# Expert outputs of a routed layer are weighted on the chip and scattered with an add into the output rows

## The reference

```python
def hier_moe(xn, w_router_group, w_router_expert, w_gate, w_up, w_down):
    t = xn.reshape(-1, D_MODEL)
    lg = (t @ w_router_group).astype(jnp.float32)
    g = jnp.argmax(lg, axis=-1)                       # one of 4 groups
    p_g = jnp.max(jax.nn.softmax(lg, axis=-1), axis=-1, keepdims=True)
    le = (t @ w_router_expert).astype(jnp.float32).reshape(-1, N_GROUPS, EXPERTS_PER_GROUP)
    le_g = jnp.einsum('nge,ng->ne', le, jax.nn.one_hot(g, N_GROUPS, dtype=jnp.float32))
    top_v, top_i = lax.top_k(le_g, TOP_K_IN_GROUP)    # two of its 8 experts
    w_sel = jax.nn.softmax(top_v, axis=-1) * p_g
    ...
    def expert_step(acc, ew):
        wg, wu, wd, cw = ew
        h = jax.nn.silu(t @ wg) * (t @ wu)
        return acc + cw[:, None] * (h @ wd).astype(jnp.float32), None
...
    return h + hier_moe(rms_norm(h, g_norm_ffn), ...)
```

## Time and profile before

| | us |
|---|---|
| median of 3 runs | 599.04 |
| profiled execution | 603.15 |
| its span | 601.5 |
| PE busy (TensorE, matmuls) | 552.0 (92%) |
| DVE (VectorE) | 278.9 (46%) |
| ACT (ScalarE) | 168.3 (28%) |
| POOL (GpSimd) | 156.6 (26%) |

### The profile page before, as it was taken

One profiled execution on the slowest core, in us unless ns is written; L12 is line 12 of the kernel. 1 busy time (PEld: TensorE's weight loads), 2 busy tenths in 40 slices (PEclk: granted clock), 3 DMA queues, 4 the chain that ended last, 5 costly groups with the idle time before them and its releaser, 6 DMA issues.

```text
span 601.5 us, 8410 instructions
## 1 busy us (share of the span) xinstructions
PE 552.0 (92%) x2972; PEld 322.4 (54%) x2972; DVE 278.9 (46%) x694; ACT 168.3 (28%) x386; POOL 156.6 (26%) x187
## 2 busy tenths in 40 slices
PE   6999999999999989999999999999987878789993
PEld 4798899897675655553555944333332223233321
DVE  5887677978314899614458631111210111111245
ACT  7445343423302647622322210100110000000013
POOL 0488788410001187610000021121110111100003
PEclk9999999999999999999999798999998899999998
DMA  7990332589586920049805759999999999999856
GB/s 277 278 289 24 121 145 79 182 250 310 180 210 200 405 104 2 3 138 392 350 35 212 278 177 379 409 420 419 421 422 420 423 417 422 420 421 419 349 225 244
DMA packets 48199, 163.48 MB, mean 272 GB/s; under 512 B 8666, under 2 KB 22042, under 8 KB 36872
## 3 DMA queue, kind: packets, MB, share of 16 engines
q1 hardware_dynamic: 41344, 144.93, 64.1%
q0 software_dynamic: 6528, 17.01, 7.8%
q10 hardware_dynamic: 288, 1.05, 0.4%
HBM read 151.06 MB, written 19.76 MB: 284 GB/s over the span
## 4 chain that ended last, share of the span: by engine, by line
PE 47%; DMA 16%; SPq 11%; DVE 7%; issue 3%; POOL 3%; ACT 3%; DVEq 0%; POOLq 0%; ACTq 0%
PE bank L1129 10%; DMA ring<-in_w_up_dram 10%; PE bank L1061 9%; SPq L533 8%; PE bank L1156 4%; DMA x<-q_rows 3%; SPq L546 3%; DMA ring<-results 2%; PE bank L1012 2%; PE bank L831 2%; POOL ring L2188 2%; PE bank L926 2%; PE bank L809 2%; PE bank L832 2%; PE bank L836 2%
## 5 line engine op out<-in xcount | busy, mean ns | idle before, releaser
L1129 PE MATMUL bank<-ring,work 128*64 128x512 f32 x512 | 121.2, 629 | 18.3 <-DMA ring<-in_w_up_dram 18.3
L1129 PEld LDWEIGHTS bank<-ring,work 128*64 128x64 f32 x512 | 39.7, 144 | 96.5 <-issue 82.4
L1506 DVE TENSOR_TENSOR work<-work,bank 128x256 f32<-128x256 f32 x16 | 6.7, 421 | 135.1 <-ACT work L1441 135.1
L752 PE MATMUL bank<-split 128*128 128x384 f32 x192 | 66.1, 344 | 0.1
L1156 PE MATMUL bank<-ring,work 128*64 128x512 f32 x256 | 58.5, 598 | 7.6 <-ACT work L1445 7.6
L753 PE MATMUL bank<-split 128*128 128x384 f32 x192 | 64.3, 335 | 0.0
L2255 POOL DMA_INDIRECT work<-hn_rows,tbl x15 | 15.2, 1016 | 107.7 <-PE bank L1139 92.4
L1441 ACT ACTIVATE work<-bank 128x256 f32<-128x256 f32 x16 | 6.1, 384 | 131.1 <-PE bank L1129 131.1
L1061 PE MATMUL bank<-ring 128*128 128x512 f32 x96 | 42.6, 595 | 0.0
L2188 POOL TENSOR_TENSOR ring<-ring 128x192 f32<-128x192 f32 (+1 forms) x40 | 38.8, 989 | 7.9 <-DVEq L1601 6.8
L2263 POOL DMA_INDIRECT results<-work,tbl x15 | 15.0, 1001 | 99.0 <-DVE work L2033 99.0
(11 more groups left out here) (277 smaller groups left out, 873.2 us busy)
## 6 DMA issues: line engine op xcount, KB each, us to landing
ring<-in_w_down_dram SPq DMA_DIRECT2D x32, 1024.0 KB
ring<-in_w_gate_dram SPq DMA_DIRECT2D x28, 1024.0 KB
ring<-in_w_up_dram SPq DMA_DIRECT2D x28, 1024.0 KB
ring<-in_w_in_dram SPq DMA_DIRECT2D x7, 1536.0 KB, 11.3
results<-work POOLq DMA_DIRECT2D x1, 4160.0 KB, 24.5
x<-in_x_prompt_dram SPq DMA_DIRECT2D x8, 512.0 KB, 15.7
ring<-in_w_out_dram SPq DMA_DIRECT2D x2, 2048.0 KB, 16.1
ring<-in_w_gate_dram SPq DMA_DIRECT2D x8, 512.0 KB, 20.6
```

Source lines behind the costliest of these rows:

```text
L752: pe.matmul(bank[n % 3][:, 0:CW], xT_high[:, k, cols], w_high[c][:, k, :], start=(k == 0), stop=False)
L1129: last = pe.matmul(bank[2][64 * h:64 * h + 64, :], xgT[:, k, 64 * h:64 * h + 64], gate_up[s][h][:, :, k, :], start=(k == 0), stop=(k == KD ...
L1506: return dve.tensor_tensor(out, a, b, op)
```

## The change

The output rows take the sum themselves. SyncE writes `x` (that is `h`) to the output right after it is complete, behind the weights of pair 2 and ahead of those of pair 3. VectorE and ScalarE multiply by the slot's weight while they copy a pair's result out of its banks. GpSimd then scatters those rows straight into the output with an add, by two indirect DMAs for a pair: one into the 512 prompt rows, which skips the sample tokens, and one into the 8 sample rows, which skips all others. Word 1 of the table is now the row in the sample output.

An add that goes out while another one to the same row is on its way would be lost. Two things prevent that. A pair now holds the experts `i` and `i + 16`, which lie in different groups, so that no token stands twice in one pair. And the scatter of a pair waits until that of the pair before has landed, and the first one until the rows of `h` have landed.

The weights of all 16 pairs' slots come from one matrix product (`weigh`, 16 columns in place of 1), which both copies of pair 0 now wait for. What goes: the tensor `results` with its clearing, its reading back, the sums of VectorE, ScalarE and GpSimd at the end, the matrix `holder` and its matmuls, the four dummy matmuls and two `own_row` products behind pair 13, and the special treatment of pair 15. The loops of VectorE and ScalarE over the pairs are written out. The weights' requests are the same DMAs in the same order, for other experts. The overflow branch is rewritten too.

```diff
@@ SyncE
-            gates((4, 5), 2, (1,))
+            gates((2, PAIRS + 2), 2, (1,))
+            for m, t in enumerate(ORDER):
+                sp.wait_ge(S["h_done"], m + 1)
+                sp.dma_start(y_rows[t] if t < NT else ys_rows, x[0:TILES[t], t, :]).then_inc(S["y_out"], 16)
+            third = (3, PAIRS + 3)
             sp.wait_ge(S["pair_half"], 1)
-            half_gates((6, 7), 0, 0, gu_in[0])
+            half_gates(third, 0, 0, gu_in[0])
...
-            combine_rows(1)
@@ TensorE
-                        last = pe.matmul(bank[7][:, 0:1], in_slot[:, i, m, :], weigh_by[:, i, m:m + 1],
+                        last = pe.matmul(bank[7][:, 0:PAIRS], in_slot[:, i, m, :], in_pair[:, i, m, :],
...
-                if i == 13:
-                    own_row(SUMMED[0], 0)
-                    own_row(SUMMED[0], 1)
-                    keep_warm(4, bank[3])
@@ ScalarE
-                act.wait_ge(S["dn_done"], i + 1)
-                act.activation(yo[s][:, 0:512], bank[4][:, :], ACT.Copy).then_inc(S["dn_evac_a"], 1)
+                if landed is not None:
+                    act.wait_ge(res_sem[s], landed)
+                else:
+                    act.wait_ge(S["tbl_ready"], 4)
+                if split:
+                    act.wait_ge(S["pair_half"], 2)
+                else:
+                    act.wait_ge(S["dn_done"], i + 1)
+                act.activation(yo[s][:, 0:512], bank[4][:, :], ACT.Copy, scale=weight).then_inc(S["dn_evac_a"], 1)
@@ VectorE
-                dve.tensor_copy(yo[s][:, 512:D], bank[5][:, :]).then_inc(S["dn_evac_v"], 1)
+                dve.tensor_scalar(yo[s][:, 512:D], bank[5][:, :], weight, None, ALU.mult).then_inc(S["dn_evac_v"], 1)
@@ GpSimd
-            pool.wait_ge(S["v_used"], 2)
-            pool.memset(xg[0], 0.0).then_inc(S["zero_rows"], 1)
-            clear_results(1)
...
-            def scatter(i, s, choices):
+            def add_rows(s, tokens, decoded):
+
+                for out, at, n in ((y_prompt[0], tokens, SEQ), (ys_rows, decoded, DEC)):
+                    pool.indirect_dma_start(out, bass.IndirectOffsetOnAxis(at, 0), yo[s], None, bounds_check=n - 1,
+                                            oob_is_err=False, compute_op=ALU.add).then_inc(res_sem[s], 16)
+
+            def scatter(i, s):
 
                 pool.wait_ge(S["dn_evac_a"], i + 1)
                 pool.wait_ge(S["dn_evac_v"], i + 1)
+                if i >= 1:
+                    pool.wait_ge(res_sem[(i - 1) % 3], 32 * ((i - 1) // 3 + 1))
                 pool.sem_inc(S["moved_go"], 1)
-                pool.indirect_dma_start(results, bass.IndirectOffsetOnAxis(choices, 0), yo[s], None,
-                                        bounds_check=CHOICES - 1, oob_is_err=False).then_inc(res_sem[s], 16)
+                add_rows(s, tbl[:, 0, i:i + 1], tbl[:, 1, i:i + 1])
...
-            pool.wait_ge(S["scattered"], 16)
-            for i in range(PAIRS - 1):
+            pool.wait_ge(S["y_out"], 16 * (NT + 1))
+            for i in range(PAIRS):
                 if i + 4 < PAIRS:
                     pool.wait_ge(S["xg_turned"], 2 * i + 4)
                     gather((i + 1) % 3, tbl[:, 0, i + 4:i + 5])
-                scatter(i, i % 3, tbl[:, 1, i:i + 1])
+                scatter(i, i % 3)
```

More of the change, by code:

```diff
@@ L588, in _ @@
                     i = 3 * j + 6 + s
-                    expert(2 * i, 2 * i + 1, s, i)
+                    expert(i, i + PAIRS, s, i)
             sp.wait_ge(S["gu_done"], PAIRS - 3)
-            half_gates((30, 31), 0, 0, S["front_in"])
-            half_gates((30, 31), 0, 1, gu_in[0])
+            half_gates((PAIRS - 1, E - 1), 0, 0, S["front_in"])
+            half_gates((PAIRS - 1, E - 1), 0, 1, gu_in[0])
             sp.wait_ge(S["dn_done"], PAIRS - 3)
[L594 to L608, removed]
-            combine_rows(1)
+            downs((PAIRS - 1, E - 1), 0)
             sp.wait_ge(S["flag_ready"], 1)
@@ L1166, in _ @@
             weigh()
-            with pe.Fori(0, 4) as j:
+            for i in (1, 2, 3):
+                s = i % 3
+                pair(i, s, i // 3 + 1, False)
+                turn_tokens(i + 1, (s + 1) % 3, 16 * (i // 3 + 1))
+                pair_down(i, s, i // 3 + 1, False)
+            with pe.Fori(0, 3) as j:
                 for n, s in enumerate((1, 2, 0)):
-                    i = 3 * j + 1 + n
-                    turn = j + 1 + (1 if s == 0 else 0)
+                    i = 3 * j + 4 + n
+                    turn = j + 2 + (1 if s == 0 else 0)
                     pair(i, s, turn, False)
-                    turn_tokens(i + 1, (s + 1) % 3, 16 * (j + 1) + (16 if s == 0 else 0))
+                    turn_tokens(i + 1, (s + 1) % 3, 16 * (j + 2) + (16 if s == 0 else 0))
                     pair_down(i, s, turn, False)
-            def own_row(t, half):
-                pe.matmul(sum_bank(t, half)[:, :], ident[:, :], x[:, t, half * 512:(half + 1) * 512], start=True, stop=False)
             for i in range(13, 16):
@@ L1183, in _ @@
                     turn_tokens(i + 1, (s + 1) % 3, 80)
-                else:
-                    own_row(SUMMED[1], 0)
                 pair_down(i, s, i // 3 + 1, False, i == PAIRS - 1)
-                if i == 13:
-                    own_row(SUMMED[0], 0)
-                    own_row(SUMMED[0], 1)
-                    keep_warm(4, bank[3])
[L1192 to L1195, removed]
-                for half in range(2):
-                    if m == 0:
-                        pe.wait_ge(S["dn_evac_v" if half else "dn_evac_a"], PAIRS)
-                    if t == 3:
-                        pe.wait_ge(*((S["h_done"], T5 + 1) if half else (S["add_read"], 1)))
-                    pe.matmul(sum_bank(t, half)[0:TILES[t], :], holder[:, t, 0:TILES[t]], yo[0][:, half * 512:(half + 1) * 512],
-                              start=(t not in SUMMED), stop=True).then_inc(S["added"], 1)
             pe.wait_ge(S["flag_ready"], 1)
@@ L1868, in read_ranks @@
                 for m in range(m0, m1):
-                    at_ = chain.put(tt(place_in[:, m, :], rank(b, m - m0)[:, 0:2], away[:, m, :], ALU.add))
+                    at_ = chain.put(tt(place_in[:, m, :], rank(b, m - m0)[:, 0:E:PAIRS], away[:, m, :], ALU.add))
                 for m in range(m0, m1):
@@ L2042, in _ @@
-            with dve.Fori(0, 3) as j:
-                for n, s in enumerate((1, 2, 0)):
-                    i = 3 * j + 4 + n
-                    hidden(i, False)
-                    tokens(i + 1)
-                    result(i, s, 16 * (j + 1) + (16 if s == 0 else 0))
-            for i in range(13, 15):
-                hidden(i, False)
-                tokens(i + 1)
-                if i == 14:
-                    for t in range(T5):
-                        dve.tensor_scalar(holder[:, t, :], iota128, float(t * P), last_token, ALU.add, ALU.is_equal)\
-                            .then_inc(S["slot_ready"], 1)
-                result(i, i % 3, 16 * (i // 3))
```

206 lines of the change are left out of this document (65 added, 141 removed).

## The result

The kernel after takes **603.62 us** (median of 11 runs, 601.16 to 606.21); the kernel before, run beside it, took 598.43 (11 runs). The ratio is 1.0095, 95% interval 1.0067 to 1.0122: slower by about 0.9%. The forecast was 602.7 us and 0.6% slower. Two of the 12 executions of the kernel with the clearing put back (611.84 and 899.29 us) and one of the 12 of the kernel before with its clearing later (2542.65 us) were in a slow state, of which the cause isn't known, and the ratios leave them out.

What follows compares the result with a forecast made beforehand. The DMA engines were taken to bound the pairs' stage. Tail -10.1, clock +1.2, add +10.9, skipped rows +1.0 and rows of `h` +0.7 gave +3.7 us, a median of 602.7 us; range 591.5 to 613, 8 in 10.

Steps and rivals of the forecast that it cites:

- What bounds the kernel: Pairs' stage, 352 to 568 us: DMA engines always busy at 410 GB/s, so bytes added there lengthen the kernel in full.
- The add: Pairs' scatters: an add costs one row time more, 13 x 0.65 x 1.28 = +10.9 us (0 to 21.8).
- The tail: Behind the last down product: copy, scatter, landing and 0.8 us closing, new end 591.4, -10.1 us (-12 to -9).
- TensorE's clock: Pair 14's gate and up: without the dummies 8.78 us, not 7.09; partly covered by waiting, +1.2 us (0 to 1.7).
- Skipped rows: Scatters into the sample rows: skipping nearly all 128 slots, 13 times, costs +1.0 us (0 to 2).
- The rows of `h`: Writes of 2.1 MB before pair 3's weights: idle engines at 341 to 351 us hide them, +0.7 us (0 to 4).
- At nothing: Parts put at no cost: the clearing, pair 0's copies waiting for `weigh`, scaled copies, GpSimd's second issue, written-out loops.
- The chain of scatters: Rival, chance 0.10: each scatter waits for the one before; at 16 us a cycle the time is 616.
- The sum: Whole kernel: -10.1 + 1.2 + 10.9 + 1.0 + 0.7 = +3.7 us, span 605.2, median 602.7 us, 0.6% slower.

Runs made afterwards that it cites:

- The run with SyncE's wait: The kernel after, with the wait for the last scatters moved from GpSimd to the end of SyncE's program: 601.12 us, ratio 1.0035.
- the doubled writes: The kernel after, with the rows of `h` written once more, 2.1 MB to a spare tensor: 605.53 us, ratio 1.0099.

## Why the prediction was right, by its steps

**What bounds the kernel** held. Taking the add out shortened the stage by 10.8 us, which is no less than what it took of the engines ahead of pair 14's weights (13 x 0.73 = 9.5 us), and making TensorE faster in pair 14 left the stage as long as it was (238.80 us against 238.70).

**The add** (+10.9) is the term that decided, and its size was right: 10.8 us of stage between the two traces, 9.9 to 10.9 with the other traces. Its factors were each a little off: 0.73 us for a scatter, not 0.65. With 13 scatters that is 9.5 us of the mean engine, so the factor for the busiest one would be 10.8/9.5 = 1.14 and not 1.28, if the whole 10.8 are the add's. No run measured that factor by itself.

**The tail** (-10.1) was wrong by half: -4.7. I had the last landing at 590.6, 8.5 us behind the last down product, and the end 0.8 later. What it measured behind that product: the first scatter issued at +1.7, forecast +1.6; the second one issued 1.85 after it, because an issue with an add takes 1.55 us; the landing of that one 4.3 us after its issue, shorter than the 6.93 that I took from the copy, and than my lower end of 5, for which I had shown no row; then 6.8 us of closing for 0.8. The step that failed is "the span ends at 601.5, so 0.8 us": I read the closing of before, where GpSimd was done with its sums at 588.40 + 4.99 = 593.39 and could take its branch while others worked, as a property of the end, though the change puts the flag and the branch behind the last landing. The run with SyncE's wait shows 4.0 us of it; the 2.0 us by which the other 2.8 exceed my 0.8 stay open.

**TensorE's clock** (+1.2): pair 14 took 9.81 us, more even than 8.78, but a faster one is worth some 0.5 us at most in the runs. I had let only 0.5 us of waiting cover it; where the stage ends by its weights, the next wait takes up all of it.

**Skipped rows** (+1.0): q0's share with copies alone rose from 8.4% to 9.2%, 2.1 us, of which 0.25 MB more, mostly pair 15's rows, are 0.6; the other 1.5 us go with 16 more scatters, like the 1.6 us above. Leaving them out gave 0.7 us in time by the medians. That is within my range of 0 to 2, and too small for the runs to size.

**The rows of `h`** (+0.7): nothing that can be told, as the doubled writes show. `tokens(0)` waited for its tile but started sooner than before, so did pair 3's requests (348.55, was 351.95).

**At nothing.** The copies of pair 0 did wait for the weights of the rows, without harm: VectorE's started at 360.15, in before at 361.02. The clearing was not nothing, but -1.3 us (put back in the kernel after) to -2.1 us (moved in the kernel before) at the first product of the output projection; a miss of mine, since I looked at whom GpSimd waits for later and not at what the late start had cost by then.

**The chain of scatters** fell, but not by much at first. Waits of POOL from 340 to 602 us (total, times, longest):

```profile
POOL out_dram L2130 <- DMA out_dram<-work,tbl: 41.6, 6, 7.8
```

Six pairs, 2 to 7, waited for the scatter before, then GpSimd caught up, and no other engine waited for it. The kernel without the second scatter had no such wait and was hardly faster. The pairs came closer together there than the 15.1 us that I had averaged: the scatters of pairs 2 and 3 went out at 390.36 and 402.79, 12.4 us apart.

**The sum.** The forecast's outcome, 602 to 606 us, had a chance of 0.25, and its mechanism, an add at one row time more, is what the runs show. That the total also came out within 1 us is in part luck, because errors met. In the spans the tail gave 5.4 us less than I said; the stage grew by 8.5 us and not by 10.9 + 1.2 + 1.0 = 13.1, 4.6 less; the start moved by -3.4 and not by +0.7, 4.1 less: 3.7 + 5.4 - 4.6 - 4.1 = +0.4. The medians differ by 5.2 because the execution of before that I worked from was itself 4.7 us above its median. Of the start's -3.4 us, 1.8 are there at the output projection (257.13 against 258.95); the rest is no more than executions differ by, since pair 0 starts anywhere from 342.92 to 346.58 in the traces of the kernels after without the clearing. Part of that lies in the stage: from pair 0's start to the last down's end it took 233.85 us, but 578.36 - 346.21 = 232.2 in the kernel before with the later clearing, and 231.6 with plain copies. The clock's and the skipped rows' terms are not to be seen beside such a spread. What made that execution longer stays open.

## What to carry to other kernels

In a stage that is bound by the DMA engines, count an accumulating scatter as twice its rows. Here it removed a read-back of 4.2 MB and a sum behind the bound, which gave 4.7 us, and put 10.8 us inside it. When a wait is moved to the end of a queue, look at what stands behind it there: a flag load and a branch behind the last landing cost 4.0 us in the traces (2.5 by the medians), and another engine could wait. Bulk clearing belongs where the DMA engines are idle and not beside a load that someone waits for: moving it gave 1.4 us.

## What the runs showed of the hardware

The issue of an indirect DMA takes GpSimd longer with an add. Instructions of the scatter by tile (ns min/median/max, first and last start) and its landings, for the kernel after and for the one without the add:

```profile
L2130 POOL DMA_INDIRECT out_dram<-work,tbl x32: 1552/1559/1621, 361.8 to 590.8; - x32
...
DMA to landing us min/median/max: 4.3/9.6/11.7
```

```profile
L2130 POOL DMA_INDIRECT out_dram<-work,tbl x32: 974/986/1016, 359.9 to 577.5; - x32
...
DMA to landing us min/median/max: 3.0/8.2/9.9
```

That is 0.57 us more for each issue, and 1.4 us more to the landing as a median of both scatters, far from the 4.8 us that the chain would have needed.

The stretches at half of TensorE's clock (1.2 instead of 2.4 GHz) lie in other places from one execution to the next, and keeping TensorE busy in one place didn't keep a later product fast. The last down product took 3.65 us in the kernel after (granted clock 1.00), 6.38 with the dummies behind pair 13 (0.57), and 6.37 with the clearing put back (0.58), which changes nothing near it. In the five traces in which it took 5.12 us or more, TensorE had waited 1.8 to 2.4 us for the last down weights just ahead; in four of the five with 3.65 us it had waited 0.5 to 1.03 us there, but in the kernel with SyncE's wait 2.41. Such a product is no place to read a small difference from one trace.
